# A hybrid attention and RWKV-7 backbone: a load is issued earlier in the transfer queue, and a half of the last dense pass is left out

## The reference, cut to what matters

```python
u_ctx = h_ctx @ w_in[:, :STATE_CH]              # the context needs no receptances and no gates
u_lat = h_lat @ w_in                            # keys, values, low ranks, receptances r, gates
z = token_shift(u_lat[..., :CONV_CH], shift_w)  # three taps over the tokens
...
for d in range(N_DIR):                          # forward and backward, the state from the context
    def step(s, inp):
        sa = einsum('bhvk,bhk->bhv', s, kk_t)
        s = s * w_t - sa * (kk_t * a_t) + v_t * k_t
        y = einsum('bhvk,bhk->bhv', s, r_t)
...
return (o.astype(gate.dtype) * silu(gate)) @ w_out
```

## Time and profile before

| what | value |
|---|---|
| median of three runs | 4954.7 us (4951.6 to 4957.8) |
| the profiled execution, its own time | 4968.3 us, span 4966.4 |
| PE, PEld busy | 4625.1 us (93%), 2742.7 us (55%) |
| DVE, ACT, POOL busy | 2674.7 (54%), 1796.5 (36%), 1378.9 (28%) |
| mean granted clock of TensorE | 0.97 of full speed |
| L2268, the dense products | 2048 PE instructions, 486.8 us busy |
| L2050 and L2052, GpSimd's inversion | 1008 each, 310.7 and 320.1 us busy |
| `keep_rw_hg`, the latents' load | 64 transfers of 1024 KB |
| `keep_gate`, the spreads | 576 transfers of 64 KB |
| a 64 KB store of y, issue to landing | 2.9 us (median) |

### The profile page before, as it was taken

One profiled execution on the slowest core, in us unless ns is written; L12 is line 12 of the kernel. 1 busy time (PEld: TensorE's weight loads), 2 busy tenths in 40 slices (PEclk: granted clock), 3 DMA queues, 4 the chain that ended last, 5 costly groups with the idle time before them and its releaser, 6 DMA issues. The chain is left out here.

```text
span 4966.4 us, 120707 instructions
## 1 busy us (share of the span) xinstructions
PE 4625.1 (93%) x48510; PEld 2742.7 (55%) x48510; DVE 2674.7 (54%) x4780; ACT 1796.5 (36%) x4413; POOL 1378.9 (28%) x2884
## 2 busy tenths in 40 slices
PE   6999996999999999899999997999998999999699
PEld 3666663333333333454444444787777778878544
DVE  2444443655666654232143345766666667666476
ACT  1222221444444343033122223555555555555332
POOL 1111111323322331000000002555555455555343
PEclk8999997999999999899999998999999999999799
DMA  5222223000000002533412235677676666777575
GB/s 215 94 85 98 85 77 127 4 25 24 25 25 24 25 6 96 218 136 114 117 62 65 76 94 154 173 185 176 167 181 166 166 174 169 188 175 174 150 228 177
DMA packets 938529, 585.99 MB, mean 118 GB/s; under 512 B 659125, under 2 KB 882997, under 8 KB 923960
## 3 DMA queue, kind: packets, MB, share of 16 engines
q1 hardware_dynamic: 851514, 556.33, 38.3%
q10 hardware_dynamic: 86528, 22.82, 2.1%
HBM read 382.11 MB, written 196.88 MB: 117 GB/s over the span
## 5 line engine op out<-in xcount | busy, mean ns | idle before, releaser
L934 PE MATMUL at_bS<-at_qT,at_kT 97*64 97x512 f32 (+1 forms) x2368 | 607.0, 598 | 15.1 <-ACT at_pT L1032 14.5
L1645 PE MATMUL p_bU<-keep_hT,p_slab 128*128 128x512 f32 (+1 forms) x1504 | 591.3, 554 | 12.8 <-DMA p_slab<-in_o_w_in_dram 7.4
L1069 DVE TENSOR_REDUCE at_mx<-at_bM 128x1 f32<-128x512 f32 (+1 forms) x656 | 394.2, 628 | 353.8 <-PE at_bM L899 352.9
L2268 PE MATMUL rw_bank<-keep_rw_hg,rw_slab 128*128 128x256 f32 x2048 | 486.8, 392 | 22.4 <-DMA keep_rw_hg<-scratch_hT 22.4
L1032 ACT ACTIVATE at_pT<-at_bS 128x512 f32<-128x512 f32 (+1 forms) x592 | 342.5, 591 | 398.2 <-PE at_bS L934 378.8
L1645 PEld LDWEIGHTS p_bU<-keep_hT,p_slab 128*128 128x128 f32 x1504 | 286.6, 191 | 311.0 <-issue 282.7
L2268 PEld LDWEIGHTS rw_bank<-keep_rw_hg,rw_slab 128*128 128x128 f32 x2048 | 385.9, 193 | 88.9 <-DMA keep_rw_hg<-scratch_hT 24.9
L856 POOL TENSOR_TENSOR at_sum_pool<-at_sum_pool,at_pT 128x512 f32<-128x512 f32 x192 | 244.2, 1272 | 372.1 <-ACT at_pT L1032 354.7
L2052 POOL TENSOR_TENSOR rw_g_at<-rw_g_at,rw_g_prod 64x14 f32<-64x14 f32 (+6 forms) x1008 | 320.1, 318 | 79.0
L2050 POOL TENSOR_TENSOR rw_g_prod<-rw_g_at 64x14 f32<-64x14 f32 (+6 forms) x1008 | 310.7, 308 | 79.1
L934 PEld LDWEIGHTS at_bS<-at_qT,at_kT 97*64 97x64 f32 x2368 | 155.5, 137 | 279.8 <-issue 187.5
(11 more groups left out here) (288 smaller groups left out, 9624.5 us busy)
## 6 DMA issues: line engine op xcount, KB each, us to landing
keep_wide<-scratch_heads SPq DMA_DIRECT2D x144, 512.0 KB, 4.6
keep_rw_hg<-scratch_hT SPq DMA_DIRECT2D x64, 1024.0 KB
keep_gate<-scratch_inverses SPq DMA_DIRECT2D x576, 64.0 KB
scratch_bv<-keep_wide SPq DMA_DIRECT2D x144, 128.0 KB
scratch_products<-rw_NB SPq DMA_DIRECT2D x288, 64.0 KB
scratch_y<-rw_ysb ACTq DMA_DIRECT2D x288, 64.0 KB, 2.9
scratch_heads<-p_z SPq DMA_DIRECT2D x17, 1024.0 KB, 4.9
m_yin<-scratch_y SPq DMA_DIRECT2D x32, 512.0 KB, 5.6
```

The costliest lines, as they stand in the source:

```text
L934: last = pe.matmul(bS[rows, g % 3, 0:nq * P], kT[:, s, k * P + VH * x:k * P + VH * x + VH], qT[:, s, q0 * P:(q0 + nq) * P], start=True, st ...
L1069: nc.vector.tensor_reduce(mx[:, j, piece:piece + 1], bM[:, (FIRST_ITEM[b] + i) % 2, 0:n], AX.X, ALU.max).then_inc(max_red, 1)
L1645: last = pe.matmul(bU[:, n % 4, 0:w], slab[:, i, k, :], hT[:, k, tok:tok + w], start=(k == 0), stop=(k == KD - 1))
L2268: last = pe.matmul(DENSE[:, GT * half:GT * (half + 1)], slab[:, half, q, :], hg[:, x.slot, q, :], start=(q == 0 and half == 0), stop=(q == ...
```

## The change

In SP's order `dense_before(n)` moves from behind `gather` to ahead of `keep_inverses`; with it go the slabs' two transfers at the start of a pass. In TensorE's `dense`, a pass without receptances returns from half 0 after its waits, and half 1 starts the bank's accumulation itself.

```diff
                     load(n.on(5), 1)
                     keep_products(n.on(3), 1)
+                    dense_before(n)
                     keep_inverses(n.on(2))
                     gather(n.on(3))
-                    dense_before(n)
                     spread(n.on(2))
                     dense_behind(n)
...
                         pe.wait_ge(hg_l[x.slot], 16 * (x.t // 2 + 1))
                         pe.wait_ge(slab_l, 32 * (x.on + 1))
                         pe.wait_ge(dn_out, x.t)
+                        if not x.queries:
+                            return
                     for q in range(KD):
                         last = pe.matmul(DENSE[:, GT * half:GT * (half + 1)], slab[:, half, q, :], hg[:, x.slot, q, :],
-                                         start=(q == 0 and half == 0), stop=(q == KD - 1), skip_group_check=True)
+                                         start=(q == 0 and (half == 0 or not x.queries)), stop=(q == KD - 1), skip_group_check=True)
```

## The result

The changed kernel takes 5052.6 us (median of four runs, 5045.5 to 5062.7), the one before 4953.9 beside it: a ratio of 1.020, 95% interval 1.018 to 1.022. It is slower by 99 us where 14 us of gain were forecast.

What follows compares the result with a forecast made beforehand. The RWKV stage's chain copy, matmul, copy, state sets the pace together with a busy PE; 6.7 + 0 + 6 + 2.5 - 1.3 = 13.9 us off 4954.7 gives about 4941 us, range 4919 to 4966.

Steps and rivals of the forecast that it cites:

- 56 usual bodies: 0, on the edge of three covers: In 56 usual bodies the earlier load costs 0: delays to spreads, gather and SP are just covered by slack.
- Rival B: Unexplained PE stalls in the RWKV stage shift: half gone gives 4921, as many more 4961; chance 0.10 each.
- issue: PE idle that no operation explains, some 39 us in the RWKV stage; moving over 20 us makes the forecast wrong.
- Rival A: Usual bodies: inverses or gather land over 5 us later, far_p waits and GpSimd holds SP; 4973 us, chance 0.15.
- not 5.5 to 6.5: Sign of being right: spreads of a usual body start 5.5 to 6.5 us behind the inverses instead of 3.4.
- signs of being wrong: far_p waiting in usual bodies, SP waiting for GpSimd by tens of us, last-pass r1 intervals over 5.5, burst beside small transfers.
- Pass starts: At seven pass starts the dense products' wait for the load goes: gain about 6 us, bounds 14 and -6.
- What was late next: At pass starts far_p then waits for the spread, some 2.5 us in the second pass.
- First bodies: At the stage's first bodies PE's 2.31 us load wait shrinks: gain 2.5 us, at most 3.2 before spreads limit.
- Part 1: No receptances in the last pass: eight bodies lose dense half 0, gain 6.7 us, bounds 9.4 and -1.5.
- C: PE sets the pace, so the skipped halves bring 29.8 us and the pass starts 17.5: 4907 us, chance 0.05.
- D: Gain handed over entirely to far_p waits at pass starts and clock falls in the last pass: 4951 us, chance 0.22.

Runs made afterwards that it cites:

- the runs with the half moved: Dense half 1 one chunk earlier in changed kernel (1.032) and kernel before (1.028); in next body, kernel before: 1.025, with 128 KB load 1.021.
- the skip alone: Kernel before with only the last pass's receptances left out, the latents' load in its old place: ratio 0.999 to the kernel before.
- the load between: Changed kernel with the load one step later in SP's order, between inverses and gathering: ratio 1.005 to the kernel before.
- all loads early: Last pass's receptances left out, every load issued first in SP's body, right behind the bonus store: ratio 1.011 to the kernel before.

## Why the prediction was wrong

**The step that failed** is "56 usual bodies: 0, on the edge of three covers". It cost 58.6 us in the 46 bodies outside the last pass. The covers that it names are not the main reason; a fourth, which it does not have, was used up: the lead of PE's own instructions. PE's instructions themselves come over the DMA engines, and where PE starts 60 to 80 instructions in a us (matmuls and weight loads), a packet is due every 3 to 4 us. The load had stood over the one stretch in which PE needs few; moved, it lies behind and over a fast one, and PE has begun some 440 instructions since the last packet started when it stops. That the moved bytes cost, and that the long stalls end on a packet of instructions, the longest on one that starts as the burst ends, the runs and traces show; that the fast stretch ahead is what uses the lead up is argued from the runs with the half moved. The prediction priced what stands behind the moved transfer in its queue, and not what runs beside its bytes.

**Rival B** named the symptom, "issue", and the prediction had the test: wrong as a whole if "issue" moves by more than 20 us. It moved by 59. B was given as half or double of the 39 us, without a mechanism, and so its price was a guess, 4961 where 5053 came. The 59 us are also not all: behind a long stall the granted clock falls to 0.50, as in the windows of 3772 to 3774, and PE works at it for a while when it resumes: slow, though "busy". Against the run with the skip alone PE's idle time in the stage rises by 55 us (50 of issue, 15 of `far_p`, less 9.5 of waits for the load), and its busy time by 30 (1489.6 against 1459.9). Most of the 30 is the clock: 22 stretches at 0.50 take 117.5 us, in 98.9 of which PE is busy, against 12 stretches, 58.0 and 49.5 us, with the skip alone. By an estimate from these, work at half the clock taking twice as long at most, that is up to 25 us. The 20 fetch gaps are 60 us long together, the 4 with the skip alone 10.

**Rival A** is there, but small. The inverses do queue behind the load: spreads start 7.2 us behind them at 3502.14 (6.2 to 9.8 over the bodies with a load), not 5.5 to 6.5, and SP's gather takes 3.6 and 4.3 us to issue. SP's timeline of the usual body beside the earlier trace rows:

```profile
3501.43 0.60 SPq L1971 DMA_DIRECT2D keep_rw_hg<-scratch_hT  x1
3502.14 0.38 SPq L1944 DMA_DIRECT2D scratch_inverses<-rw_g_out  x1
3503.93 3.56 SPq L1935 DMA_DIRECT2D rw_g_in<-scratch_products  x1
3507.55 0.48 SPq L1935 DMA_DIRECT2D rw_g_at<-scratch_products  x1
3509.33 5.77 SPq L1957 DMA_DIRECT2D keep_gate<-scratch_inverses  x8
```

Yet of `far_p`'s 21.4 us only one wait, of 1.2, stands in a usual body; 11.8 are at five pass starts, 2.6 at the first body and 5.7 at the end. GpSimd did come to hold SP, 27.5 us in 25 times against 10.4 in 4, which was on the prediction's list of signs of being wrong; but in the run with the load between it held it by 3 us in 57 bodies, for 0.5%.

**Pass starts**: a gain of 6 was forecast, a loss of 9.3 came (189.3 us instead of 180.0 over all seven, though the last one also lost its half). The wait for the load went, 13.7 us, as forecast. What was late next was named rightly, and was a little dearer:

```profile
3426.76 0.51 PE L2154 MATMUL rw_bank<-keep_gate,rw_NB 64*64 64x64 f32 x10 [3.24 <-DMA keep_gate<-scratch_inverses]
```

3.24 us at the second pass's start, where 2.5 stood. The rest I take to be the burst again, 2 MB of it; it was not worked out. **First bodies**: 2.5 us of gain were forecast, none came. The wait of 2.31 us for the load went, and `far_p` waits 2.61 for the spreads instead, the limit that the prediction named; the first copy of r1 comes 75.6 us behind the stage's first PE instruction, 75.0 before.

**Part 1** was near: 5 us by the times (-1 to 10) and 7.8 by the copies, where 6.7 was forecast, partly by luck. Two sizes were off and cancelled partly. The interval shrinks to 4.26 us and not to 4.79, which gives 1.7 instead of 1.18 us per body; and from the fourth copy to the next body the skip costs 0.8 (7.13 to 7.94), where only falls of the clock had been allowed for.

**Rivals C and D** did not come: no run is near 4907, and D's 4951 has no loss in it.

## What to carry to other kernels

Before a large transfer is moved, look at what the engines execute while its bytes move, not only at what queues behind it: a burst of 1 MB was free over large matmuls and cost 1.3 us per body behind and over a stretch of small ones. The number of small instructions under the burst does not decide alone: with the half moved, 58 to 69 in a us under it cost nothing more. Idle marked "issue" that is a multiple of the usual length (here up to 4.3 us instead of 1.8) is a sign to look for an instruction packet in the DMA view of that stretch. And where a wait is rare, as here at seven of 72 bodies, move only the transfer that causes it: moving the slabs alone brought some 10 us (15 with the skip), the move in all bodies cost 99 with it.

## What was unexpected of the hardware

- PE's instruction packets and bursts of data get in each other's way: in the kernel before, 8 packets start inside 59 bursts where PE's instructions there would use 15, and in the changed one 20 stalls of over 2 us end behind a packet. PE resumes 1.2 to 1.6 us behind the end of a 16 KB instruction packet that itself takes 0.93 to 1.06 us in most stalls; the longest stall was 4.5 us (4115.14).
- Instruction packets never come close together: of their spacings in the stage 99 in 100 are above 3.3 us, in every kernel looked at. With some 250 recorded instructions to a packet in this stage that is about 75 in a us (an estimate from the shortest spacings), while PE begins over 90 in a us in a tenth of the stage. A fast stretch thus lives on what is in hand, even without a burst.
- The load 2 us later in the median (the load between) took three quarters of the loss away, from 1.020 to 1.005; a load half a body away (all loads early) still cost 1.1%.
- Another queue is little protection: with the load issued by ScalarE the spreads still went out 8.6 us behind the third copy of r1, against 9.5 with it ahead of them in SP's queue and 5.4 before.
- A stall of 4 us is paid twice: the granted clock falls behind it from 1.00 to 0.50 (at 0.50 from 3772.65 to 3779.47 us, while PE resumes at 3774.90); the changed kernel has 22 stretches at 0.50 in the stage, the skip alone 12.
